# Token sums in pieces on VectorE, pair work in another order, and silu as one ScalarE function, in a hybrid decoder block

## What is computed

```python
x = x + rms_norm(merged @ w_out[l], post_mix_g[l])
h = rms_norm(x, pre_ffn_g[l])
gt, up = jnp.split(h @ w_ffn_in[l], 2, axis=-1)
f = (jax.nn.silu(gt) * up) @ w_ffn_out[l]
x = x + rms_norm(f, post_ffn_g[l])
```

## Time and profile before

| what | value |
|---|---|
| median of 3 runs | 741.84 us (739.65 to 742.28) |
| the profiled execution, its own time | 742.22 us |
| its span in the trace | 740.4 us |
| PE (TensorE matmul) busy | 704.9 us, 95% of the span |
| DVE busy | 540.5 us, 73% |
| ACT busy | 349.3 us, 47% |
| POOL busy | 206.2 us, 28% |
| mean granted TensorE clock | 0.986 |

### The profile page before, as it was taken

The page is one execution under the profiler, slowest core; times in us unless marked ns, Lnnn a source line. Parts: engine busy times, 40 slices in busy tenths (PEclk is TensorE's granted clock), DMA queues, the critical chain, the costliest instruction groups (busy, mean ns, idle before and its releaser), DMA issues.

```text
span 740.4 us, 11196 instructions
## 1 busy us (share of the span) xinstructions
PE 704.9 (95%) x3944; PEld 615.5 (83%) x3944; DVE 540.5 (73%) x765; ACT 349.3 (47%) x567; POOL 206.2 (28%) x180
## 2 busy tenths in 40 slices
PE   5999999999999999999999999999999995699996
PEld 4788888888888888888898899999999994488885
DVE  5428877678576566893759488888888889877677
ACT  6325534544545463242534354445444553266663
POOL 2042211122210002740250353344334409600003
PEclk9999999999999999999999999999999998799999
DMA  6349899989883214237103213312332242255663
GB/s 239 115 139 252 207 227 218 249 240 223 217 219 96 98 58 143 87 112 255 58 30 124 105 58 114 113 68 102 113 113 76 94 170 80 90 173 199 196 198 129
DMA packets 37752, 107.31 MB, mean 145 GB/s; under 512 B 4083, under 2 KB 4083, under 8 KB 37532
## 3 DMA queue, kind: packets, MB, share of 16 engines
q1 hardware_dynamic: 29708, 83.86, 33.1%
q0 software_dynamic: 8000, 23.07, 14.6%
q10 hardware_dynamic: 16, 0.02, 0.0%
HBM read 104.82 MB, written 25.19 MB: 176 GB/s over the span
## 4 chain that ended last, share of the span: by engine, by line
PE 65%; DVE 17%; issue 9%; ACT 4%; DMA 1%; POOL 1%; DVEq 1%; SPq 0%; ACTq 0%; POOLq 0%
PE bank L1544 20%; PE bank L1546 20%; PE bank L1545 20%; DVE g_lo L1371 4%; DVE s_lo L1459 2%; ACT blk_hi L844 2%; DVE w_lo L1443 2%; DVE ff_silu L1324 2%; DVE raw_pair L1377 1%; ACT ff_tanh L828 1%; PE bank L1595 1%; DVE blk_lo L1371 1%; DMA x_tok<-in_x_dram 1%; DVE g_sum L1436 1%; PE bank L1585 1%
## 5 line engine op out<-in xcount | busy, mean ns | idle before, releaser
L1544 PE MATMUL bank<-h_hi,w_hi 128*128 128x512 f32 (+1 forms) x424 | 162.0, 382 | 1.8 <-DVE h_lo L1014 1.8
L1546 PE MATMUL bank<-h_hi,w_lo 128*128 128x512 f32 (+1 forms) x424 | 160.1, 378 | 0.0
L1545 PE MATMUL bank<-h_lo,w_hi 128*128 128x512 f32 (+1 forms) x424 | 160.0, 377 | 0.0
L986 DVE TENSOR_TENSOR w_lo<-raw,w_hi 128x1024 fp32r<-128x1024 f32 x58 | 77.1, 1329 | 56.1 <-ACT w_hi L596 46.5
L1544 PEld LDWEIGHTS bank<-h_hi,w_hi 128*128 128x128 f32 x424 | 79.8, 188 | 16.1 <-issue 2.2
L1546 PEld LDWEIGHTS bank<-h_hi,w_lo 128*128 128x128 f32 x424 | 79.8, 188 | 14.9
L1545 PEld LDWEIGHTS bank<-h_lo,w_hi 128*128 128x128 f32 x424 | 79.9, 188 | 13.9
L1544 PE MATMUL bank<-w_hi,s_hi 128*128 128x512 f32 x154 | 62.7, 407 | 14.8 <-DVE s_lo L1459 14.8
L1443 DVE TENSOR_TENSOR w_lo<-raw,w_hi 128x1024 fp32r<-128x1024 f32 (+1 forms) x39 | 55.9, 1433 | 22.9 <-ACT w_hi L874 22.9
L874 ACT ACTIVATE w_hi<-raw 128x1024 fp32r<-128x1024 f32 (+1 forms) x39 | 40.9, 1048 | 55.1 <-PE bank L1546 55.1
L1545 PE MATMUL bank<-w_lo,s_hi 128*128 128x512 f32 x154 | 62.1, 403 | 0.0
(11 more groups left out here) (234 smaller groups left out, 1693.9 us busy)
## 6 DMA issues: line engine op xcount, KB each, us to landing
raw<-in_w_in_dram SPq DMA_DIRECT2D x42, 512.0 KB, 4.7
raw_pair<-in_w_ffn_in_dram SPq DMA_DIRECT2D x36, 512.0 KB, 3.6
comb<-in_w_ffn_out_dram POOLq DMA_DIRECT2D x30, 512.0 KB, 7.6
raw<-comb SPq DMA_DIRECT2D x20, 512.0 KB, 3.6
raw<-in_w_ffn_out_dram SPq DMA_DIRECT2D x15, 512.0 KB, 3.9
comb<-comb POOLq DMA_DIRECT2D x10, 512.0 KB, 5.1
raw<-in_w_branch_dram SPq DMA_DIRECT2D x8, 512.0 KB, 3.2
raw<-in_w_out_dram SPq DMA_DIRECT2D x8, 512.0 KB, 3.3
```

The costliest lines, as they stand in the source:

```text
L986: dve.tensor_tensor(dst, src_hi[0], src_hi[1], ALU.subtract).then_inc(lo_done, 1)
L1544: pe.matmul(dst, a_hi, b_hi, start=start, stop=False, skip_group_check=resumed)
L1545: pe.matmul(dst, a_hi, b_lo, start=False, stop=False, skip_group_check=resumed)
L1546: return pe.matmul(dst, a_lo, b_hi, start=False, stop=stop, skip_group_check=resumed)
```

## The change

Three edits.

1. **Token sums.** POOL's eight instructions for `s1` to `s4` are gone. VectorE makes them in 24 pieces of two k-tiles (one for the last piece of each), one piece in each unit from n = 2 on (`token_sum`), in the order s3, s2, s1, s4. The phases of the down product go in another order, P1, P2, P4, P6, P7, P5, P3, so that P4, which needs no sum, comes third. P6, P5 and P3 now accumulate on P1's banks, and c21, c22 and c12 are gathered otherwise: `C11_MADE, C21_PART, C21_MADE, C22_MADE = 26, 28, 30, 35` say in which unit. In the units 32 and 33 TensorE does all of the first token tile before the second (`turned`), since P3 goes on in the banks which ACT copies at the end of P5. The products with the gain for c11, c21 and c22 go from DVE to POOL (six instructions, 128x512). The output tiles 2 and 3 are finished first.
2. **Order of pair work on DVE.** `pair_end(n - 1)` stands in pair n, after the group 3 and group 0 splits; `last_weight_sum` comes after `u22`, no longer before it; the group 2 split comes after the second `g_sum` addition.
3. **Silu.** ACT makes `ff_silu` with its `Silu` function, into two buffers; DVE's `silu_part` is gone, and the factor 0.5 with it.

```diff
-PH_P1, PH_P2, PH_P6, PH_P5, PH_P7, PH_P3, PH_P4 = range(7)
-DOWN_BANKS = [(0, 1), (2, 3), (0, 1), (4, 5), (0, 1), (4, 5), (0, 1)]
-DOWN_FIRST = (PH_P1, PH_P2, PH_P5)
-SUM_SPLIT = 6
+PH_P1, PH_P2, PH_P4, PH_P6, PH_P7, PH_P5, PH_P3 = range(7)
+DOWN_BANKS = [(0, 1), (2, 3), (6, 7), (0, 1), (4, 5), (0, 1), (0, 1)]
+DOWN_FIRST = (PH_P1, PH_P2, PH_P4, PH_P7)
+PIECES = (FF_HALF + 1) // 2
...
@@ block.gpsimd @@
-            pool.wait_ge(u_read, FF_TILES)
-            pool.wait_ge(prod_done, PRODUCTS * FF_PAIRS)
...
-                pool.tensor_tensor(s3[:, ks, :], f11[:, ks, :], f21[:, ks, :], ALU.add).then_inc(f_summed, 1)
...
+            pool.wait_ge(gain_full, 48)
+            for i, (c, half) in enumerate(((c11, 0), (c21, 0), (c22, 1))):
+                for t in range(2):
+                    pool.wait_ge(sq_done, 16 + 2 * i + t + 1)
+                    pool.tensor_tensor(c[:, t, :], c[:, t, :], gain[:, half * SEQ:(half + 1) * SEQ], ALU.mult)\
+                        .then_inc(c_gained, 1)
...
@@ block.scalar @@
-            def ff_tanh_part(j, src):
-                if not isinstance(j, int) or j >= 1:
-                    act.wait_ge(g_read, j)
-                act.activation(ff_tanh[:, :], src, ACT.Tanh, scale=0.5).then_inc(tanh_done, 1)
+            def ff_silu_part(j, q, src):
+                if not isinstance(j, int) or j >= 2:
+                    act.wait_ge(u_read, j - 1)
+                act.activation(ff_silu[:, q, :], src, ACT.Silu).then_inc(silu_done, 1)
...
+                if n == C11_MADE + 1:
                     for t in range(2):
                         act.wait_ge(c_made, 1 + t)
-                        square_sum(c11[:, t, :], 44 + t, junk[:, 0:SEQ])
...
+                        square_sum(c11[:, t, :], 46 + t, junk[:, 0:SEQ])
...
@@ block.vector @@
-            def silu_part(j, src):
...
             def pair_end(n, q, jp):
...
-                silu_part(n + FF_PLAIN, g_sum[:, q, :])
...
-                dve.scalar_tensor_tensor(out=f[:, jp, TOK_HALF:], in0=ff_silu[:, TOK_HALF:], scalar=0.5,
-                                         in1=u22[:, q, :], op0=ALU.mult, op1=ALU.mult).then_inc(u_read, 1)
+                dve.tensor_tensor(f[:, jp, TOK_HALF:], ff_silu[:, q, TOK_HALF:], u22[:, q, :], ALU.mult).then_inc(u_read, 1)
...
+            def pair_steps(n, q, more, jp_done):
...
                 blocks_lo(n, 3, q)
                 if more:
                     blocks_lo(n + 1, 0, 1 - q)
-                    blocks_lo(n + 1, 1, 1 - q)
-                    last_weight_sum(n + 1, 1 - q)
...
+                if not isinstance(n, int) or n >= 1:
+                    pair_end(n - 1, 1 - q, jp_done)
+                if more:
+                    blocks_lo(n + 1, 1, 1 - q)
                 dve.wait_ge(prod_done, n * PRODUCTS + PR_P3)
                 dve.wait_ge(part_moved, n * 3 + 3)
                 dve.tensor_tensor(g_sum[:, q, TOK_HALF:], bank[z][:, 0:TOK_HALF], g_sum[:, q, TOK_HALF:], ALU.add)
                 dve.wait_ge(prod_done, n * PRODUCTS + PR_P7)
                 dve.tensor_tensor(u22[:, q, :], bank[x][:, 0:TOK_HALF], u22[:, q, :], ALU.add).then_inc(u22_done, 1)
                 if more:
-                    blocks_lo(n + 1, 2, 1 - q)
+                    last_weight_sum(n + 1, 1 - q)
...
                 dve.tensor_tensor(g_sum[:, q, 0:TOK_HALF], bank[y][:, 0:TOK_HALF], g_sum[:, q, 0:TOK_HALF], ALU.add)\
                    .then_inc(g_sum_done, 1)
+                if more:
+                    blocks_lo(n + 1, 2, 1 - q)
...
+            def token_sum(m):
...
+                which, piece = divmod(m, PIECES)
+                ks = slice(2 * piece, min(2 * piece + 2, FF_HALF))
+                if which == SUM_S3:
+                    dve.tensor_tensor(s3[:, ks, :], f11[:, ks, :], f21[:, ks, :], ALU.add).then_inc(f_summed, 1)
...
             for n in range(2, DOWN_UNITS):
...
                 down_lo(n)
                 s_lo_part(n)
...
+                if n - 2 < 4 * PIECES:
+                    token_sum(n - 2)
+                if n == C11_MADE:
                     dve.wait_ge(p_moved, 2)
                     dve.wait_ge(unit_done, in_ring(U_DOWN) + down_done(PH_P2))
...
+                    add_product(c11, PH_P2)
...
@@ block.tensor @@
+            turned = down_done(PH_P5) - 1
...
+                if n in (turned, turned + 1):
+                    for t in range(2):
+                        if n > turned:
+                            pe.wait_ge(p_moved, 5 + t)
+                        for i, (ph, k) in steps:
+                            ins = down(n, i, ph, k, t)
```

More of the change, by code:

```diff
@@ L102, in down_split_count, with sum_count @@
     return sum(len(down_loads(m)) for m in range(n + 1))
+C11_MADE, C21_PART, C21_MADE, C22_MADE = 26, 28, 30, 35
+def sum_count(which, k, count):
+    return which * PIECES + (k + count - 1) // 2 + 1
 def down_done(ph):
@@ L408, in _ @@
                       .then_inc(raw_full[u % RING], 16)
[L409 to L412, removed]
+            for m, t in enumerate((2, 3, 0, 1)):
+                for half in range(2):
+                    sp.wait_ge(out_ready, 2 * m + half + 1)
                     sp.dma_start(out[0, t * P:(t + 1) * P, half * SEQ:(half + 1) * SEQ],
@@ L946, in _ @@
             act.wait_ge(g_sum_done, FF_PAIRS)
[L947 removed]
+            ff_silu_part(FF_TILES - 1, 1, g_sum[:, 1, :])
             for n in range(2, DOWN_UNITS):
@@ L1469, in _ @@
-            for n in range(FF_PAIRS - 2, FF_PAIRS):
-                pair_steps(n, n % 2, n < FF_PAIRS - 1)
-                pair_end(n, n % 2, FF_HALF - 1)
-            def gained(c, t, half, sign):
-                g = gain[:, half * SEQ:(half + 1) * SEQ]
-                if sign > 0:
-                    dve.tensor_tensor(c[:, t, :], c[:, t, :], g, ALU.mult).then_inc(y_gained, 1)
-                else:
-                    dve.scalar_tensor_tensor(out=c[:, t, :], in0=c[:, t, :], scalar=-1.0, in1=g, op0=ALU.mult,
-                                             op1=ALU.mult).then_inc(y_gained, 1)
+                    pair_steps(i * 2 + q, q, True, i + (first_jp - 1 + q))
@@ L1482, in add_x1, with add_product, take_product @@
+            def add_product(c, ph):
+                for t in range(2):
+                    dve.tensor_tensor(c[:, t, :], bank[DOWN_BANKS[ph][t]][:, :], c[:, t, :], ALU.add).then_inc(c_made, 1)
+            def take_product(c, ph):
+                for t in range(2):
+                    dve.tensor_tensor(c[:, t, :], c[:, t, :], bank[DOWN_BANKS[ph][t]][:, :], ALU.subtract)\
+                       .then_inc(c_made, 1)
             def add_x1(c, i, t, half):
-                cols = slice(half * SEQ, (half + 1) * SEQ)
@@ L1510, in _ @@
-                if n == down_done(PH_P7) + 6:
-                    for t in range(2):
-                        dve.wait_ge(sq_done, 18 + t + 1)
-                        gained(c22, t, 1, 1)
-                if n == down_done(PH_P3) + 2:
-                    dve.wait_ge(unit_done, in_ring(U_DOWN) + down_done(PH_P3))
-                    for t in range(2):
-                        dve.tensor_tensor(c12[:, t, :], bank[DOWN_BANKS[PH_P3][t]][:, :], c12[:, t, :], ALU.add)\
-                           .then_inc(c_made, 1)
@@ L1519, in _ @@
-                if n == down_done(PH_P3) + 4:
-                    for t in range(2):
-                        dve.wait_ge(sq_done, 20 + t + 1)
-                        gained(c12, t, 1, -1)
+                    add_product(c11, PH_P2)
+                if n == C21_PART:
+                    dve.wait_ge(p_moved, 4)
+                    dve.wait_ge(unit_done, in_ring(U_DOWN) + down_done(PH_P4))
+                    add_product(c21, PH_P4)
+                if n == C21_MADE:
+                    dve.wait_ge(c_made, 4)
+                    dve.wait_ge(unit_done, in_ring(U_DOWN) + down_done(PH_P7))
+                    take_product(c21, PH_P7)
```

173 lines of the change are left out of this document (79 added, 94 removed).

## The result

The changed kernel takes 713.54 us (median of four runs, 712.88 to 715.35), against 741.17 us for the kernel before in the same comparison: a ratio of 0.9632, 95% interval 0.9606 to 0.9658. The forecast was 713. The profiled execution took 715.35 us, with a span of 713.5 us and a mean granted clock of 0.995.

The account below looks back on a forecast made before the run. TensorE is nearly always busy, so time is won only where it waits or runs slowly. Span 740.4 - 21.8 (down) - 7.5 (pairs) + 0.4 (gain products) = 711.5; execution 713.3, median 712.9, so 713 us; range 710.8 to 720.5.

Parts of the forecast that it names:

- The excess of 21.8 us: Down stage: 126.5 us against 104.7 undisturbed; 14.8 us of `s_lo` waits and about 7 us of slow clock, all to go.
- The 24 pieces on DVE: Down stage: one token-sum piece per unit, at most 0.68 us each, fits DVE's idle time; cost zero, bounds 0 to 2 us.
- The gain products on POOL: Down stage and end: six POOL instructions of 1.30 us can hold DVE splits; cost 0.4 us, bounds 0 to 5.
- The walk through units 26 to 32: Down stage: with gain products and bank additions, the 2.4 us of slack fall to about zero at unit 32 and return.
- `last_weight_sum` behind `u22`: Pair stage: frees 0.6 us of DVE's queue ahead of `u22`, more than the usual 0.31 us loss plus 0.10.
- rival A: Pair stage keeps its stalls, POOL's earlier sums taking silu's place: 720.5 us; chance 0.10.
- 0.8 us of stalls: Pair stage: allowance because `u22` ends 7.9 to 8.45 us into the pair and TensorE wants it at 8.64.
- Silu's table: Pair stage: if shared with Copy and Square, one more table load before the first silu, where ACT idles; cost nothing.
- Rival C: Table loaded afresh in each loop pass and after it: about 10 loads of 1.28 us, 713 to 726, say 717; chance 0.06.
- Rival D: Pair stage: Silu's table lacks Copy, two loads a pair delay `u22`: 729 us, bounded above by 754; chance 0.05.
- The stated point at which the case turns slow: Pair stage, two table loads a pair: slower than the kernel before from 1.65 us a load all told.
- Rival B: Down stage keeps part of its loss, gain products holding splits in units 27 to 38: 716 to 720 us; chance 0.09.

## Why the prediction was right, and where it was not

**The down stage** went as worked out. The excess of 21.8 us was POOL's sums holding DVE's splits, and the slow clock that followed; 20.2 us of it went with them. Of the 1.6 us left, 1.2 are the stall below, and 0.4 us more is left in the kernels without that stall (105.1 against the 104.7 worked out). The run with useless work on POOL shows that it was the work and not its result that TensorE waited for. The 24 pieces on DVE cost nothing, as forecast: they run until unit 25, and TensorE is busy 44.0 of 44.0 us in the first stretch, with no two matmuls more than 0.24 us apart up to that unit.

**The gain products on POOL** were mis-sized: "I take 0.4 us for both", and they cost 1.2 us, within the stated bounds of 0 to 5. The walk through units 26 to 32 held: no matmul there comes more than 0.1 us late. The step that failed was near the end, where only the reciprocal roots and the last additions were looked at. In unit 35 DVE adds c22's two banks, and directly after that POOL's two products and the small instruction hold two splits, so that the split of unit 37 ends 1.1 us late. Moved off POOL, the stall is gone.

**The pair stage** came out at 182.6 us, forecast 183.0, but the reason was only half right. The prediction gave the gain to two edits: `last_weight_sum` behind `u22` as "more than the usual loss in a pair", and silu. The runs with one edit undone:

| pair stage, us | tanh and DVE step | Silu |
|---|---|---|
| old order | 188.9 | 183.8 |
| new order | 190.0 | 182.6 |

Silu gives 5.1 us in the old order and 7.4 in the new one. The order gives 1.2 us with Silu (0.9 in the last two profiles), nearly all of it in the first pair or in a wait at P6 that came once. With tanh it gains nothing: its stage is 1.0 us longer, in one trace of each kernel, and the times don't separate the two (720.54 to 721.01 against 719.22 to 721.49 us). So the step of the prediction that failed here is the worth of `last_weight_sum` behind `u22`: with tanh it buys nothing, and with Silu the usual pair waits for nothing in either order. (The 190.5 us of the kernel before and the 188.9 us of the same order here differ mostly by three pairs that lost 1.0, 0.7 and 1.2 us in its profile, where silu had met a POOL sum just started and took 1.59, 1.23 and 1.72 us; in the run here no silu step took over 1.13 us.) The waits and the timeline of tanh in the new order show where the 0.6 us went that `last_weight_sum` freed; TensorE's waits in the pairs (total us, times, longest), then DVE, PE, ACT and POOL:

```profile
PEld bank L1552 <- DVE u L1431: 6.0, 12, 0.8
...
PEld bank L1552 <- ACT g_sum L916: 1.1, 4, 0.3
```

```profile
482.40 2.22 DVE L1372 TENSOR_TENSOR g_lo<-raw_pair,g_hi 128x1024 fp32r<-128x1024 f32 x1
484.54 1.78 DVE L1372 TENSOR_TENSOR blk_lo<-raw_pair,blk_hi 128x512 fp32r<-128x512 f32 x1
486.24 0.68 DVE L1325 SCALAR_TENSOR_TENSOR ff_silu<-ff_silu,g_sum 128x512 f32<-128x512 f32 x1
...
489.30 0.41 DVE L1431 TENSOR_TENSOR u<-bank,u 128x256 f32<-128x256 f32 x1
489.63 1.77 DVE L1378 TENSOR_TENSOR raw_pair<-raw_pair,w_sum 128x512 f32<-128x512 f32 x1
...
489.76 0.39 PE L1552 MATMUL bank<-tm_hi,g_hi 128*128 128x256 f32 x1 [0.31 <-DVE u L1431]
...
494.41 0.39 PE L1552 MATMUL bank<-tm_hi,blk_hi 128*128 128x256 f32 x1
...
491.56 1.06 ACT L844 ACTIVATE blk_hi<-raw_pair 128x1024 fp32r<-128x1024 f32 x1 [5.06 <-PE bank L1554]
492.53 0.61 ACT L828 ACTIVATE ff_silu<-g_sum 128x512 f32<-128x512 f32 x1
493.05 1.04 ACT L844 ACTIVATE g_hi<-raw_pair 128x1024 fp32r<-128x1024 f32 x1
494.00 0.36 ACT L916 ACTIVATE g_sum<-bank 128x256 f32<-128x256 f32 x1
...
489.57 1.28 POOL L545 TENSOR_TENSOR w_sum<-raw_pair 128x512 f32<-128x512 f32 x1 [3.80 <-DMA raw_pair<-in_w_ffn_in_dram]
```

TensorE loses time in two ways. The first is the old one, P4 waits for `u22` (489.76). Silu itself is no longer held up (0.68 us; 0.69 to 1.72 before), but POOL's sums, which come earlier now, hold `g_lo` and the group 0 split ahead of it (2.22 and 1.78 us). In the pairs 3 to 14 (of 0 to 17) the group 0 and group 2 splits take 1.40 us in the mean, against 0.95 in the old order with tanh, and DVE's instructions in a pair add up to 9.9 us against 9.6. This is what rival A described, POOL's sums in silu's place. The second is new, at P6 (494.41, in four pairs). `last_weight_sum`, now behind `u22`, meets POOL's first weight sum and takes 1.77 us. ACT's group 2 copy waits for it by the program (it starts at 491.56, 0.16 us after its end, though the view names another releaser). Tanh, `g_hi` and the copy of P1 stand behind that copy in ACT's program, and P6 waits for the last of them, which ends at 494.36. What `last_weight_sum` freed ahead of `u22` was taken up by the splits that POOL holds and by ACT's queue behind it. This is read from the timeline; no run moves POOL's sums alone. With Silu the queue ahead of `u22` is 0.9 us shorter: the step's 0.68 us, and 0.23 us that the product behind it waited for it. In the changed kernel, DVE again:

```profile
491.65 1.78 DVE L1367 TENSOR_TENSOR g_lo<-raw_pair,g_hi 128x1024 fp32r<-128x1024 f32 x1 [0.46 <-ACT g_hi L844]
493.35 1.79 DVE L1367 TENSOR_TENSOR blk_lo<-raw_pair,blk_hi 128x512 fp32r<-128x512 f32 x1
...
496.24 1.23 DVE L1367 TENSOR_TENSOR blk_lo<-w_sum,blk_hi 128x1024 fp32r<-128x1024 f32 x1 [0.44 <-ACT blk_hi L844]
497.38 0.42 DVE L1419 TENSOR_TENSOR g_sum<-bank,g_sum 128x256 f32<-128x256 f32 x1
497.76 0.42 DVE L1421 TENSOR_TENSOR u<-bank,u 128x256 f32<-128x256 f32 x1
```

It idles 0.44 us for ACT before group 1, and `u22` ends at 498.18, about 0.8 us ahead of P4; the walk had it 0.2 to 0.7 ahead, "tight", and kept 0.8 us of stalls which didn't come. The first pair kept 1.0 us where 0.8 were forecast. So rival A, POOL's earlier sums in silu's place, didn't come in the changed kernel: the sums do meet `g_lo` and group 0 (1.78 and 1.79 us), but with Silu DVE has the time; with tanh they cost what the order had won.

**Silu's table** holds Copy and Square: the changed kernel loads twice in all, at the start and once before the first silu, where ACT idled anyway. Silu on 128x512 takes 0.615 us, against 0.633 for tanh, but the order makes that difference and not the function: tanh in the new order takes 0.616 us, and Silu in the old one 0.632. Rival C didn't come. Rival D didn't either, and its price was too low: 738.6 us measured where 729 was worked out, since the wait that ends last is another one, P6's for ACT's copy of P1.

By the Trainium skill ("ScalarE: Activation LUTs", What ACT_TABLE_LOAD costs) a load takes 1283 ns and a drain of 1.38 us comes with each switch. The trace has the 1283 ns to the nanosecond, but not the drain: 0.02 us lie between the copy and the load, and the 778 us estimated with it are 39 too many.

The stated point at which the case turns slow (1.65 us a load) was also off. The 3.0 us that are left to the kernel before (741.63 less 738.6), shared by the 35 loads that the run has more, are 0.09 us each, so the point lies at about 1.4 us if the loss grows with the load; that is an estimate and wasn't run.

**Rival B** came in small: the down stage kept 1.2 us, not 3 to 7.

**Luck.** That the total lies within 1 us of the forecast is partly luck. In the second profile of the changed kernel the down stage is 1.2 us longer than forecast, the pair stage 0.4 us shorter, and the start of the pairs came 0.5 us earlier than in the profile that the sum started from: the three nearly cancel, and the span is 711.7 us where the sum had 711.5. The pair stage came near its figure with a wrong share for one of its two edits.

## What to carry to other kernels

Before an elementwise step goes to a free GpSimd, look at what VectorE does meanwhile: if its instructions have two SBUF operands and somebody waits for them, the free engine isn't free. A step on the path can be better on VectorE itself, in pieces put into the idle time of each round.

When a wait is removed from the front of a queue, follow what moves behind it on the other engines too; undo each edit alone, and both together, before giving it a share of the gain.

Before a new activation function is used, look at the number of table loads in the trace. Here one, where ACT idled, cost nothing, and two in each pair of 10 us cost 1.4 us a pair.

## What was not expected of the hardware

The table load shows no drain beside it: with 35 loads more, each of 1.283 us, nearly every one starts 0.02 us behind the instruction before it and ends 0.01 us ahead of the next. With the overlaps that are lost, two switches cost 2.7 us of ACT in the pair shown.

Short GpSimd instructions are slowed by VectorE in turn: the first of the 24 pieces took 1.29 us, and all of them beside VectorE's splits 43.4 us, 1.8 us each. The eight long ones took 29.9 us in the run with useless work and 30.6 us before, beside VectorE's work both times, so what they take alone isn't shown. The timelines look as if the two engines took turns, one instruction each, so that the one with the longer instructions gets most of the time; how the chip does it isn't shown.
